# The opening of a hybrid decoder layer: identity products while PE waits, tile pairs in turn, first weights in two pieces

## The reference, cut to what matters

```
def rms_norm(x, gain):
    x32 = x.astype(jnp.float32)
    y = x32 * lax.rsqrt(jnp.mean(x32 * x32, axis=-1, keepdims=True) + NORM_EPS)
    return (y * gain.astype(jnp.float32)).astype(x.dtype)
...
    proj = h @ w_in
    c_q, c_kv, k_r, fq, fk, fv, f_logit, u, gate_logits = jnp.split(proj, split_points, axis=-1)
...
        h = rms_norm(x, attn_norm_g[l])
        x = x + mixer_block(h, cos, sin, w_in[l], ...)
        h = rms_norm(x, ffn_norm_g[l])
        x = x + conv_gated_ffn(h, w_up[l], ffn_conv_w[l], w_down[l])
```

## Time and profile before

| what | value |
|---|---|
| median of 3 timed runs | 1488.74 us (1486.61 to 1490.23) |
| span of the profiled execution | 1487.9 us |
| PE busy | 1443.8 us, 97% of the span |
| DVE, ACT, POOL busy | 1003.4, 651.2, 127.2 us |
| PE's first work, first product | 7.88 us, 15.45 us |
| mean granted TensorE clock | 0.998 of 2.4 GHz |

### The profile page before, as it was taken

How to read it: one execution, slowest core, us unless ns; L and a number is a source line. 1 busy time by engine, 2 the same in 40 slices (tenths; PEclk the granted TensorE clock), 3 DMA queues, 4 the chain that set the end, 5 groups by cost and what they waited for, 6 DMA issues and landing times.

```text
span 1487.9 us, 18903 instructions
## 1 busy us (share of the span) xinstructions
PE 1443.8 (97%) x7090; PEld 1209.9 (81%) x7090; DVE 1003.4 (67%) x1378; ACT 651.2 (44%) x1054; POOL 127.2 (9%) x104
## 2 busy tenths in 40 slices
PE   7999999999999999998999999999999999999999
PEld 6999987777878777886788888888888888888887
DVE  5212366765676766856855688877877777679786
ACT  6230235554435553125632265555555555444332
POOL 1000141001420003011200000000000000000000
PEclk9999999999999999999999999999999999999999
DMA  7201231104021103226672222222222221891222
GB/s 255 67 1 75 64 92 43 37 29 147 26 84 48 33 29 100 73 64 219 211 262 85 71 62 95 85 85 79 77 86 85 85 86 49 313 388 71 85 79 78
DMA packets 129941, 148.93 MB, mean 100 GB/s; under 512 B 11002, under 2 KB 94893, under 8 KB 129581
## 3 DMA queue, kind: packets, MB, share of 16 engines
q1 hardware_dynamic: 129664, 147.67, 30.0%
q10 hardware_dynamic: 189, 0.08, 0.0%
HBM read 110.83 MB, written 36.31 MB: 99 GB/s over the span
## 4 chain that ended last, share of the span: by engine, by line
PE 52%; DVE 6%; issue 1%; ACT 1%; DMA 1%; POOL 0%; DVEq 0%; ACTq 0%; SPq 0%
PE ps L1876 28%; PE ps L2183 5%; PE ps L2185 5%; PE ps L2184 4%; PE ps L2753 2%; PE ps L2754 2%; PE ps L2755 2%; PE ps L540 2%; DVE plain_arena L2279 1%; PE ps L2272 1%; DMA plain_arena<-in_w_branch 1%; PE ps L2785 0%; DVE plain_arena L2543 0%; DMA plain_arena<-in_w_out 0%; DVE plain_arena L1047 0%
## 5 line engine op out<-in xcount | busy, mean ns | idle before, releaser
L1876 PE MATMUL ps<-split_arena 128*128 128x512 f32 x1320 | 306.8, 389 | 0.0
L540 PE MATMUL ps<-split_arena 128*128 128x512 f32 x1152 | 293.2, 402 | 6.0 <-PEq L1117 2.1
L1876 PEld LDWEIGHTS ps<-split_arena 128*128 128x128 f32 x1320 | 247.5, 188 | 51.4 <-issue 0.3
L540 PEld LDWEIGHTS ps<-split_arena 128*128 128x128 f32 x1152 | 210.2, 190 | 48.2 <-issue 8.2
L2059 ACT ACTIVATE down_ops<-down_all 128x1024 fp32r<-128x1024 f32 x77 | 81.5, 1061 | 115.5 <-PE ps L2185 115.3
L1876 PE MATMUL ps<-up_b,split_arena 128*128 128x512 f32 x528 | 126.5, 389 | 0.0
L2078 DVE TENSOR_TENSOR down_ops<-down_all,down_ops 128x1024 fp32r<-128x1024 f32 x77 | 94.1, 1223 | 46.2 <-ACT down_ops L2059 46.0
L2183 PE MATMUL ps<-down_ops 128*128 128x512 f32 x308 | 119.9, 389 | 0.5 <-DVE down_ops L2078 0.5
L2185 PE MATMUL ps<-down_ops 128*128 128x512 f32 x308 | 119.8, 389 | 0.0
L2184 PE MATMUL ps<-down_ops 128*128 128x512 f32 x308 | 119.8, 389 | 0.0
L1876 PEld LDWEIGHTS ps<-up_b,split_arena 128*128 128x128 f32 x528 | 99.1, 188 | 20.6
(11 more groups left out here) (359 smaller groups left out, 2510.8 us busy)
## 6 DMA issues: line engine op xcount, KB each, us to landing
plain_arena<-in_w_in SPq DMA_DIRECT2D x24, 512.0 KB, 4.2
scr_gate<-plain_arena SPq DMA_DIRECT2D x48, 256.0 KB, 2.0
plain_arena<-scr_gate SPq DMA_DIRECT2D x24, 512.0 KB, 4.3
plain_arena<-in_w_up SPq DMA_DIRECT2D x22, 512.0 KB, 5.1
up_raw<-in_w_up SPq DMA_DIRECT2D x22, 512.0 KB, 4.7
scr_act<-plain_arena SPq DMA_DIRECT2D x22, 512.0 KB, 2.7
down_all<-scr_act SPq DMA_DIRECT2D x18, 512.0 KB, 8.8
down_all<-in_w_down SPq DMA_DIRECT2D x18, 512.0 KB, 10.3
```

Source lines behind the costliest of these rows:

```text
L540: mm = nc.tensor.matmul(m.ps[:, self.banks[half], :], w[:, k, :], src[:, k, h * BANK:(h + 1) * BANK], start=(j == 0), stop=(j == self.PER_ ...
L1876: mm = nc.tensor.matmul(o, self.w[j][w][:, k, :], self.h[j][k][h], start=(j in self.OPENS and k == 0 and n == 0), stop=(k == self.HK - 1 a ...
```

## The change

- PE waits for the identity alone (a new semaphore, raised by a small memset of POOL behind it) and then multiplies the identity by itself `WARM` = 18 times into PSUM bank 7. Only then does it wait for the small vectors.
- The first four fills are made by pairs of tiles: tiles 0 and 1 are turned into the left half of the four banks, their high and low parts are made in pieces of 256 columns, and PE runs the products of tiles 0 and 1 for k = 0 to 3. Then tiles 2 and 3 do the same, each of their steps with one of fills 4 to 7 behind it. From k = 4 on, all four tiles go together as before. The pieces are numbered: 0 to 7 are the half-width ones, fill n of before is number n + 4 from there on.
- The first half of the weights is loaded and split in two pieces of two k each, between the loads of tiles 1, 2 and 3.
- The squares of tiles 1 and 3 are summed by DVE (`square_mean`: one multiply with a sum, which gives the mean at once) instead of ACT.
- The counts that others wait for move with it.

The core of the diff:

```
+    def square_mean(self, dve, i, junk):
+        self.m.nc.vector.tensor_tensor_reduce(out=junk, in0=self.rows[:, i, :], in1=self.rows[:, i, :], scale=1.0 / D, scalar=EPS,
+                                              op0=ALU.mult, op1=ALU.add, accum_out=self.ssq[:, i:i + 1]).then_inc(self.ms_done, 1)
...
-    def turn_first(self, pe):
-        for j in range(4):
+    def turn_pair(self, pe, pair):
+        for j in (2 * pair, 2 * pair + 1):
             pe.wait_ge(self.scaled, j + 1)
...
+            rows_in(0), rows_in(1)
+            first_weights(0)
+            rows_in(2)
+            first_weights(1)
+            rows_in(3)
             weights(0, 1)
...
+            nc.gpsimd.memset(m.stat[:, 56:57], 0.0).then_inc(ident_made, 1)
...
+            pe.wait_ge(ident_made, 1)
+            for _ in range(WARM):
+                nc.tensor.matmul(m.ps[:, 7, 0:P], m.ident[:], m.ident[:], start=True, stop=True)
...
-            nrm.turn_first(pe)
+            for pair in range(2):
+                nrm.turn_pair(pe, pair)
+                for k in range(HALF):
+                    pe.wait_ge(nrm.done, 4 * pair + k + 1)
+                    if pair == 0 and k % 2 == 0:
+                        pe.wait_ge(w_lo_done, k // 2 + 1)
+                    if pair == 0 and k == 0:
+                        pe.wait_ge(vec_done, 2)
+                    for t in (2 * pair, 2 * pair + 1):
+                        product(0, t, k, 4 + t)
+                    if pair:
+                        nrm.turn(pe, [k + 4])
             for half in range(2):
                 if half:
                     nrm.turn(pe, range(KD + 4, 2 * KD))
-                for k in range(KD):
+                for k in range(0 if half else HALF, KD):
...
-            for i in range(4):
-                act.wait_ge(x_in[i], 16)
-                nrm.square(act, i)
+            act.wait_ge(x_in[0], 16)
+            nrm.square(act, 0)
+            split_first(0)
             act.wait_ge(vec_done, 2)
-            split(0, 0)
             nrm.hi(act, range(2))
+            act.wait_ge(x_in[2], 16)
+            nrm.square(act, 2)
+            split_first(1)
+            nrm.hi(act, range(2, 8))
             split(0, 1)
-            nrm.hi(act, range(2, 4))
...
-            norms(0, 2)
+            nrm.mean(dve, 0)
+            square_mean(1)
+            nrm.scale(dve, 0)
             dve.wait_ge(vec_turned, 1)
...
-            norms(2, 4)
+            nrm.scale(dve, 1)
+            split_first(0)
             dve.wait_ge(vec_done, 2)
-            split(0, 0)
             nrm.lo(dve, range(2))
+            nrm.mean(dve, 2)
+            square_mean(3)
+            nrm.scale(dve, 2)
+            split_first(1)
+            nrm.lo(dve, range(2, 4))
+            nrm.scale(dve, 3)
+            nrm.lo(dve, range(4, 8))
             split(0, 1)
-            nrm.lo(dve, range(2, 4))
             norms(4, 6)
```

More of the change, by code:

```diff
@@ L194, in turn @@
             if n >= 4:
[L195 removed]
+                pe.wait_ge(self.done, n + 1)
             for j in range(4):
@@ L199, in turn, with spot, hi, lo @@
             t.then_inc(self.turned, 1)
-    def hi(self, act, fills):
-        for n in fills:
-            half, k = divmod(n, KD)
-            act.wait_ge(self.turned, n + 1)
-            self.m.nc.scalar.activation(self.m.h_hi[:, k, half * BANK:(half + 1) * BANK], self.m.ps[:, n % 4, :],
-                                        ACT.Copy, scale=self.gain[:, k:k + 1]).then_inc(self.hi_done, 1)
-    def lo(self, dve, fills):
-        for n in fills:
-            half, k = divmod(n, KD)
-            cut = slice(half * BANK, (half + 1) * BANK)
-            dve.wait_ge(self.hi_done, n + 1)
-            self.m.nc.vector.scalar_tensor_tensor(out=self.m.h_lo[:, k, cut], in0=self.m.ps[:, n % 4, :], scalar=self.gain[:, k:k + 1],
+    def spot(self, e):
+        if e < 8:
+            pair, n = divmod(e, 4)
+            cut = slice(pair * 2 * P, (pair + 1) * 2 * P)
+            return n, cut, self.m.ps[:, n, cut]
+        half, k = divmod(e - 4, KD)
+        return k, slice(half * BANK, (half + 1) * BANK), self.m.ps[:, (e - 4) % 4, :]
+    def hi(self, act, turns):
+        for e in turns:
+            k, cut, src = self.spot(e)
+            act.wait_ge(self.turned, e + 1)
+            self.m.nc.scalar.activation(self.m.h_hi[:, k, cut], src, ACT.Copy, scale=self.gain[:, k:k + 1]).then_inc(self.hi_done, 1)
+    def lo(self, dve, turns):
+        for e in turns:
+            k, cut, src = self.spot(e)
+            dve.wait_ge(self.hi_done, e + 1)
+            self.m.nc.vector.scalar_tensor_tensor(out=self.m.h_lo[:, k, cut], in0=src, scalar=self.gain[:, k:k + 1],
                                                   in1=f32(self.m.h_hi[:, k, cut]), op0=ALU.mult, op1=ALU.subtract).then_inc(self.done, 1)
@@ L237, in stage_load_norm_project @@
     w_lo = [cols(m.R, at + KD * NW, KD, NW) for at in w_at]
-    raw_in = [m.sem(f"pw_in{i}") for i in range(2)]
+    raw_in, first_in = [m.sem(f"pw_in{i}") for i in range(2)], m.sem("pw_first_in")
     w_hi_done, w_lo_done, prod, out_act, out_dve = (m.sem(n) for n in ("pw_hi", "pw_lo", "p_prod", "p_act", "p_dve"))
@@ L270, in weights, with first_weights, rows_in @@
                 if c >= 1:
-                    sp.wait_ge(w_lo_done, 2 * (c - 1) + half + 1)
+                    sp.wait_ge(w_lo_done, 2 * (c - 1) + half + 2)
                 sp.dma_start(raw[half][:, :, 0:n], w_src[:, HALF * half:HALF * half + HALF, first:first + n]).then_inc(raw_in[half], 16)
-            for i in range(4):
+            def first_weights(q):
+                ks, n = slice(2 * q, 2 * q + 2), chunks[0][1]
+                sp.dma_start(raw[0][:, ks, 0:n], w_src[:, ks, 0:n]).then_inc(raw_in[0] if q else first_in, 16)
+            def rows_in(i):
                 sp.dma_start(nrm.rows[:, i, :], m.ins["x"][0, i * P:(i + 1) * P, :]).then_inc(x_in[i], 16)
-            weights(0, 0)
+            rows_in(0), rows_in(1)
[3 more added lines that the diff above has]
+            rows_in(3)
             weights(0, 1)
             for i in range(4, TT):
-                sp.dma_start(nrm.rows[:, i, :], m.ins["x"][0, i * P:(i + 1) * P, :]).then_inc(x_in[i], 16)
+                rows_in(i)
             at = 0
@@ L336, in _ @@
                     nrm.turn(pe, range(KD + 4, 2 * KD))
[L337 to L343 removed]
+                for k in range(0 if half else HALF, KD):
+                    pe.wait_ge(nrm.done, half * KD + k + 5)
+                    if half == 0 and k == HALF:
+                        pe.wait_ge(w_lo_done, 3)
                     for j in range(4):
@@ L425, in split @@
                 n = chunks[c][1]
-                dve.wait_ge(w_hi_done, 2 * c + half + 1)
+                dve.wait_ge(w_hi_done, 2 * c + half + 2)
                 hi = w_hi[c % 2][:, HALF * half:HALF * half + HALF, 0:n]
@@ L436, in norms, with split_first, square_mean @@
                     nrm.scale(dve, i)
-            norms(0, 2)
+            def split_first(q):
+                ks, n = slice(2 * q, 2 * q + 2), chunks[0][1]
+                dve.wait_ge(w_hi_done, q + 1)
+                nc.vector.tensor_tensor(w_lo[0][:, ks, 0:n], raw[0][:, ks, 0:n], f32(w_hi[0][:, ks, 0:n]), ALU.subtract).then_inc(w_lo_done, 1)
+            def square_mean(i):
+                dve.wait_ge(x_in[i], 16)
+                nrm.square_mean(dve, i, cols(m.R, 31744, D))
+            nrm.mean(dve, 0)
+            square_mean(1)
+            nrm.scale(dve, 0)
             dve.wait_ge(vec_turned, 1)
@@ L612 @@
 EDGE, EDGE_LAST = 10, 4
+WARM = 18
 OPENING = (6, 9)
```

45 lines of the change are left out of this document (21 added, 24 removed).

## The result

| | median us | lowest to highest | runs |
|---|---|---|---|
| before | 1488.61 | 1486.61 to 1490.23 | 6 |
| changed kernel | 1495.14 | 1490.97 to 1497.26 | 6 |

The ratio is 1.0043 (95% interval 1.003 to 1.0055): slower by 0.43%, where 1487.9 us and no measurable difference had been forecast. Two more groups of runs gave 1.0024 (1.0009 to 1.0038) and 1.0042 (1.003 to 1.0055). The profiled execution has a span of 1493.5 us against 1487.9.

What follows compares the result with a forecast made beforehand. PE, busy 97% of the span, was taken as the bound. Of some 6.4 us (3.5 + 2.9) gained, five return in four waits: 1487.9 - 0.8 + 0.8 (median over profile) = 1487.9 us, range 1485.0 to 1491.4.

Steps and rivals of the forecast that it cites:

- Identity products: Opening of PE: 18 products start near 1.8 us, clock rises after 6.0 us of work, through at 8.6 (7.2 to 9.2).
- Square pass: DVE's new multiply of a tile by itself with a sum: 1.4 us, bounds 0.79 and 2.6.
- DVE becomes the bound: Rival, opening: DVE's square pass costs 2.6 us, not 1.4; 1490.3, up to 1492.5 with a fallen clock; chance 0.08.
- First product: PE's first product in the opening starts at 11.9 instead of 15.45, 3.5 us earlier.
- Clock in the hole: Opening, PE between 8.6 and 16.4: under 3.5 us of work, 2.2 us silent before step three; clock may fall to 1.2 GHz.
- the identity products do nothing: Rival, opening: clock stays low until products run, steps one to four slow but partly under DVE's line; +0.6, 1488.5; chance 0.05.
- the first rival: The clock falls in PE's opening hole, making steps three and four and the transposes slower; +1.2, so 1489.1; chance 0.32.
- Further waits: PE's later waits in the opening, after the 2.2 us one: 1.1 us to 20.5, then 0.9 and 0.8.
- POOL's power: Opening: tile 2's power on POOL falls beside DVE's square pass and is delayed 0.4 us, bounds 0 and 0.4.
- Net of the opening: The fill at 31.79 comes at 31.0: net -0.8 us, of some 6.4 gained five handed back in four new waits.
- Everything behind it is the same work at the same clock: After the fill forecast at 31.0: later stages unchanged, so nothing is added to the net of -0.8 us.
- if the stages behind 60 us do not simply move with it: Sign that the forecast is wrong: stages behind 60 us should only shift with the opening's last fill, forecast at 31.0.

Runs made afterwards that it cites:

- before_ident18: The kernel before with only the 18 identity products added at its start, under cover of the loads; 1491.93 us, ratio 1.0021 to before.
- before_short: The kernel before with the stores of the gate copies in the S5 stage writing 128 of 512 columns; 1489.69 us, ratio 1.0014 to before.

## Why the prediction was wrong, by its own steps

- *Identity products*: through at 7.46, forecast 8.6 between 7.2 and 9.2. The clock rose at 4.8, after 3.0 us of them, and not after the 6.0 us of work that I had taken from one row. In the six profiles with before's opening it rose 2.9 to 6.1 us behind the first product, so one row was no measure.
- *Square pass*: 1.23 and 0.08, forecast 1.4; the "DVE becomes the bound" rival was never near.
- *First product*: 11.42, forecast 11.9. Right.
- *Clock in the hole*: it fell, but at 11.6, ahead of the hole, since PE had stood still three times from 8 on (0.69, 0.30, 0.90). The products of steps one and two were slow, so the hole before step three was 0.53 us and not 2.2: the slow products lay under DVE's line, as "the identity products do nothing" had it. In the executions with the other course the hole was 2.04 to 2.09 us and the clock fell at it, which is the first rival, hole and fall.
- *Further waits*: 0.76 before 20.30 (forecast 1.1), 0.33 near 27 (0.9), 0.37 before the fill (0.8). I overpriced the hand-overs between ACT and DVE by about 0.4 each.
- *POOL's power*: I took 0.4 us of delay. The two powers took 2.28 to 2.30 us from the start of the first to the end of the second, and DVE's next scaling started 0.43 behind the read of the sum, released by the first. That first one took 1.48 us from 6.60 on, where the earlier trace rows has 0.55 for one alone, and ended 0.4 behind the square pass. The Trainium skill (SBUF — State Buffer, section "Who interferes with whom") has such an operation kept out for the whole pass. The trace agrees: both first powers, started at 6.60 and 12.44 inside the passes of 6.44 and 12.27, end some 0.4 us past them.
- *Net of the opening*: -1.5 us at the fill, forecast -0.8; level with before in the executions with the other course, where the first rival had +0.4. The forecast lies between the two. But all of this is measured against one profile of before. At 50 us the six profiles with before's opening lie from 1.3 us ahead of that one to 0.7 behind (mean 0.4 ahead), the six with the changed opening from 1.6 to 0.1 ahead (mean 0.8). So the gain of the opening is nearer 0.4 than 1.5, and these twelve don't tell it from nothing.
- **The step that failed**: "Everything behind it is the same work at the same clock." It is the same work, at another clock. I had the evidence in the earlier trace rows: silences of 1.7 to 2.4 us of which two led to 1.2 GHz and two did not. I read it as a risk for the new hole of the opening only, and not as later silences whose outcome was open in every execution, with 1.5 us at stake in each. The sum put that at nothing. Measured: five falls behind 340 us instead of two in the first profiles, four in the two others, a clock of 0.994 instead of 0.998 over all runs (some 4 to 5 us by the price above), and a late copy that with its fall costs 2.6 to 3.0. What I know now would put two to three falls (1.1 to 1.5 each) and a longer wait of 1.0 on top of 1487.9: 1491 to 1493.4, with a range that reaches past the measured 1495.14.
- *The identity products* were the second half of that step. I let them act in the opening alone. They brought 3 us to the kernel before (1.0021) with no other change. How is open.
- *The range*: its upper end took in only mishaps of the opening. None of my rivals let the change touch a later stage, though I had written that I would be wrong "if the stages behind 60 us do not simply move with it".
- *What the part without the products is worth*: 1.0003 and 1.0007, within the bound. So for the pair order, the split weights and DVE's squares the forecast of "same" holds, with no gain at the end that can be measured. Their profiles are 0.9 and 1.3 us ahead at 50 us, no more than profiles of before with the same opening are among themselves.

## What to carry to other kernels

This kernel is PE-bound to 97%, and still has silences that cost the clock in one execution and not in the next. Before forecasting an edit to the opening of such a kernel, list every silence of PE over 1.5 us with the granted clock behind it, and give the total a term for those whose outcome may change. Warm-up products under cover of the first loads looked free by every row of the opening and cost 3 to 6 us here (before_ident18 and the changed kernel). Measure them apart from whatever they come with, and read the mean granted clock of all runs, since it told the two halves of this change apart where one profile could not. And take more than one profile of the kernel before: its own opening moved by 2 us between them, more than the gain that was forecast.

## What the runs showed of the hardware that was not expected

- TensorE went to 1.2 GHz for over 3 us behind silences of PE as short as 1.71 us (ahead of 436.81, low from 438.25) and 2.08 us (ahead of 344.90, low from 346.09). The same silence of 2.09 us at the end of MLA attention was followed by a fall in some executions and not in others (0.50 behind 563.93 in the changed kernel, 1.00 behind 564.86 in the one before).
- Three profiles of the changed kernel had their falls within 0.1 us of the same places (11.6, 438.2 to 438.3, 564.5 to 564.6, 615.7 to 615.8); two of the kernel before, 0.5 us apart in the one place they share (438.0 and 438.5).
- The clock's first rise to 2.4 GHz came 2.9 to 6.1 us behind the first product in six profiles with one and the same opening (at 18.6 in before_short, at 22.0 in before_again), and the work at 50 us lies up to 2.0 us apart in them.
- A fall costs about 1.5 us where it stands and, by the estimate above, 1.1 to 1.5 in the total.
- Between two gate copies of ACT with a 256 KB store and a 512 KB load in between, ACT stood still for 5.9 to 6.9 us in the three profiles of the changed kernel and 4.9 to 6.2 in the two of the kernel before, wherever it waited for the store.
